# Sparse attention's entry in a new order: query latent, index keys, index queries, then the second key-value tile

## The reference

```
c_q, c_kv, k_idx, w_idx = split(h @ w_in, [256, 512, 576])       # 256 + 256 + 64 + 8 columns
c_q  = rms_norm(c_q, q_norm_g);  c_kv = rms_norm(c_kv, kv_norm_g)
q     = (c_q @ w_uq)    -> 16 heads of 64
q_idx = (c_q @ w_qidx)  -> 8 index heads of 64
k_idx = layer_norm(k_idx, g, b)
for each block of 128 queries:
    score = sum over heads of w_idx * relu(q_idx . k_idx)         # keys up to the query
    idx   = the 128 keys with the largest score
    attention of the 16 heads over those keys, keys and values made from c_kv
```

## Time and profile before

| | |
|---|---|
| median of three runs | 1538.74 us |
| the profiled execution, in all | 1539.63 us |
| its span, first to last instruction | 1537.8 us |
| PE busy | 1391.5 us, 90% |
| DVE busy | 851.6 us, 55% |
| ACT busy | 533.9 us, 35% |
| mean granted clock of PE, full speed is 1 | 0.952 |
| attention's entry, first latent tile to the first masked score | 878.3 to 1004.8 us |

### The profile page before, as it was taken

How to read it: one execution, slowest core, us unless ns; L and a number is a source line. 1 busy time by engine, 2 the same in 40 slices (tenths; PEclk the granted TensorE clock), 3 DMA queues, 4 the chain that set the end, 5 groups by cost and what they waited for, 6 DMA issues and landing times. The chain is left out here.

```text
span 1537.8 us, 17933 instructions
## 1 busy us (share of the span) xinstructions
PE 1391.5 (90%) x6983; PEld 1121.7 (73%) x6983; DVE 851.6 (55%) x1384; ACT 533.9 (35%) x956; POOL 171.3 (11%) x171
## 2 busy tenths in 40 slices
PE   5798889889879999999998696889989999999997
PEld 5676767779768878887886474646767888888885
DVE  4679899647454654555545538966453323332335
ACT  2353522445342222221223434557343222221321
POOL 0013230004310000000001101220010000000002
PEclk9899999899989999999999798889999999999999
DMA  9443412110404545554532120010102223322321
GB/s 330 142 164 111 162 56 83 56 55 1 164 28 155 201 139 189 185 196 166 167 121 69 33 71 28 28 56 2 55 28 82 82 82 110 110 82 82 110 73 65
DMA packets 102854, 158.36 MB, mean 103 GB/s; under 512 B 9326, under 2 KB 74107, under 8 KB 102779
## 3 DMA queue, kind: packets, MB, share of 16 engines
q1 hardware_dynamic: 91898, 115.40, 22.6%
q0 software_dynamic: 10880, 41.95, 7.8%
HBM read 155.24 MB, written 2.10 MB: 102 GB/s over the span
## 5 line engine op out<-in xcount | busy, mean ns | idle before, releaser
L396 PE MATMUL ps<-h_hi,w_hi 128*128 128x512 f32 x960 | 389.6, 406 | 6.4 <-DVE h_lo L824 6.4
L397 PE MATMUL ps<-h_lo,w_hi 128*128 128x512 f32 x960 | 382.7, 399 | 0.0
L398 PE MATMUL ps<-h_hi,w_lo 128*128 128x512 f32 x960 | 382.2, 398 | 0.0
L380 DVE TENSOR_TENSOR w_lo<-raw,w_hi 128x1024 fp32r<-128x1024 f32 x172 | 210.7, 1231 | 265.9 <-ACT w_hi L374 265.6
L374 ACT ACTIVATE w_hi<-raw 128x1024 fp32r<-128x1024 f32 x180 | 187.9, 1049 | 150.4 <-PE ps L1935 142.9
L396 PEld LDWEIGHTS ps<-h_hi,w_hi 128*128 128x128 f32 x960 | 183.9, 192 | 50.5 <-issue 9.0
L397 PEld LDWEIGHTS ps<-h_lo,w_hi 128*128 128x128 f32 x960 | 184.0, 192 | 43.2 <-issue 1.7
L398 PEld LDWEIGHTS ps<-h_hi,w_lo 128*128 128x128 f32 x960 | 183.2, 191 | 43.6
L448 DVE SCALAR_TENSOR_TENSOR ada_acc<-ada_in,c_act,ada_acc 128x512 f32<-128x512 f32 x147 | 112.8, 768 | 3.9
L1933 PE MATMUL ps<-w_hi,g_hi 128*128 128x512 f32 x256 | 101.6, 397 | 2.6 <-DVE w_lo L380 2.6
L1800 ACT ACTIVATE g_hi<-tmp 128x512 fp32r<-128x512 f32 x44 | 27.8, 632 | 211.9 <-DVE tmp L1835 211.9
(11 more groups left out here) (369 smaller groups left out, 2059.9 us busy)
## 6 DMA issues: line engine op xcount, KB each, us to landing
raw<-in_ffn_w_in_dram SPq DMA_DIRECT2D x44, 1024.0 KB, 5.1
ada_in<-in_ada_w_dram POOLq DMA_DIRECT2D x40, 1024.0 KB, 5.6
raw<-in_ffn_w_out_dram SPq DMA_DIRECT2D x20, 1024.0 KB, 5.0
raw<-in_gdn_w_in_dram SPq DMA_DIRECT2D x16, 1024.0 KB, 5.7
ada_in<-in_ada_w_dram SPq DMA_DIRECT2D x4, 1024.0 KB, 7.3
x_t<-in_x_dram SPq DMA_DIRECT2D x2, 2048.0 KB, 9.8
early_slab<-in_ada_w_dram SPq DMA_DIRECT2D x4, 1024.0 KB, 12.4
raw<-in_gdn_w_out_dram SPq DMA_DIRECT2D x4, 1024.0 KB, 5.0
```

Of the source, the lines that this page charges most:

```text
L380: ops.tensor_tensor(lo, raw_tile(s, kc) if src is None else src, f32(hi), ALU.subtract).then_inc(lo_done, 1)
L396: nc.tensor.matmul(out_, hi[:, k, :], r_hi[:, k, :], start=k == 0, stop=False)
L397: nc.tensor.matmul(out_, hi[:, k, :], r_lo[:, k, :], start=False, stop=False)
L398: last = nc.tensor.matmul(out_, lo[:, k, :], r_hi[:, k, :], start=False, stop=k == kc - 1)
```

## The change

PE makes tiles 0 and 1 only, then the small product with the query latent's statistics after its fourth chunk, the first broadcast, tile 2 with the small transposes in its middle, the index queries (now in banks 0, 1, 3 and 6), the key transposes, and tile 3 (into bank 2) with the first six logits of block 1 between its products and two behind it. The statistics of the key-value latent (into bank 0 instead of 4) follow; its broadcast (bank 1 instead of 5) moves into `dsa_q_pe`, behind the first query tile. That tile now waits for the variance (`row_made`) and for the last split of quad `Q_DSA + 1`. The logits of block 2 move behind the fourth query tile, those of block 3 behind the fourth key tile. ACT and DVE take the same order: block 1's relus and scores stand before the key-value latent's statistics and before its last weight split. POOL waits for that split before its own four. The buffer of the index queries moves to the second half of the key buffer, and block 0's mask is copied last. The diff, cut to its core (the moved calls at the end of the programs are as told here):

```diff
-        qi_t = fixed("qi_t", [P, 4, S], at=h_base)
+        qi_t = fixed("qi_t", [P, 4, S], at=k_at + 8192)
...
+        STAT_BANK, ROOT_BANK = [4, 0], [5, 1]
...
-        LAST = {3: 4 * Q_DSA + 6, 11: 4 * Q_DSA + 8, 18: 4 * Q_DSA + 9, 19: 4 * Q_DSA + 10, 35: 4 * Q_DSA + 12}
+        LAST = {3: 4 * Q_DSA + 5, 11: 4 * Q_DSA + 8, 18: 4 * Q_DSA + 9, 19: 4 * Q_DSA + 10, 35: 4 * Q_DSA + 12}
         def proj_ready(act, t):
...
+        QI_BANK = [0, 1, 3, 6]
+
         def dsa_in_pe(pe, m):
-            for s in range(4):
+            for s in range(2):
                 pe_tile(pe, Q_DSA, s, h_hi, h_lo, ready=(lambda k: h_block_here(pe, m, k)) if s == 0 else None)
-                if s == 2:
-                    pe_stats(pe, 0, sq_lat[:, 0, :, :], LC)
             pe.wait_ge(lo_done, 4 * Q_DSA + 5)
             w = [t[:, 0, 0:DC * SMALL].rearrange("p (k n) -> p k n", n=SMALL) for t in (w_hi, w_lo)]
             for k in range(DC):
                 last = mm3(ps[0:SMALL, 6, :], w[0][:, k, :], w[1][:, k, :], h_hi[:, k, :], h_lo[:, k, :],
                            k == 0, k == DC - 1)
+                if k == 3:
+                    pe_stats(pe, 0, sq_lat[:, 0, :, :], LC)
             last.then_inc(tile_done, 1)
             pe_bcast(pe, 0)
-            pe.wait_ge(sem("small_out"), 2)
-            for b in range(NB):
-                last = nc.tensor.transpose(ps[:, 7, b * SMALL:(b + 1) * SMALL], kx_t[0:SMALL, b * P:(b + 1) * P],
-                                           ident[0:SMALL, 0:SMALL])
-            last.then_inc(sem("small_turned"), 1)
+
+            def small_turn(k):
+                if k != DC // 2:
+                    return
+                pe.wait_ge(sem("small_out"), 2)
+                for b in range(NB):
+                    last = nc.tensor.transpose(ps[:, 7, b * SMALL:(b + 1) * SMALL], kx_t[0:SMALL, b * P:(b + 1) * P],
+                                               ident[0:SMALL, 0:SMALL])
+                last.then_inc(sem("small_turned"), 1)
+
+            pe_tile(pe, Q_DSA, 2, h_hi, h_lo, ready=small_turn)
             pe.wait_ge(sem("lat_made"), LC)
             pe.wait_ge(lo_done, 4 * Q_DSA + 6)
             wq = [t[:, 1, :].rearrange("p (k n) -> p k n", k=LC) for t in (w_hi, w_lo)]
             for j in range(4):
-                pe.wait_ge(sem("sq_made"), SQ_BASE[0] + j + 1)
                 for k in range(LC):
-                    last = mm3(ps[:, j, :], wq[0][:, k, j * P:(j + 1) * P], wq[1][:, k, j * P:(j + 1) * P],
+                    last = mm3(ps[:, QI_BANK[j], :], wq[0][:, k, j * P:(j + 1) * P], wq[1][:, k, j * P:(j + 1) * P],
                                cq_hi[:, k, :], cq_lo[:, k, :], k == 0, k == LC - 1)
                 last.then_inc(tile_done if j == 3 else sem("proj_mm"), 1)
-            pe_stats(pe, 1, sq_lat[:, 1, :, :], LC)
             pe.wait_ge(sem("small_made"), 2)
             for b in range(NB):
                 last = nc.tensor.transpose(ps[:, 7, b * P:(b + 1) * P], kn[:, b, :], ident[:, :])
             last.then_inc(sem("small_mm"), 1)
-            pe_bcast(pe, 1)
-
-        def indexer_pe(pe, b):
+
+            def first_logits(k):
+                if k >= 2:
+                    indexer_logit(pe, 1, k - 2)
+
+            pe_tile(pe, Q_DSA, 3, h_hi, h_lo, before=lambda: pe.wait_ge(sem("sq_made"), SQ_BASE[1] + 1),
+                    ready=first_logits, to=2)
+            for j in (6, 7):
+                indexer_logit(pe, 1, j)
+            pe.wait_ge(sem("proj_out"), AT_QI + 1)
+            pe_stats(pe, 1, sq_lat[:, 1, :, :], LC)
+            pe.wait_ge(sem("proj_out"), AT_QI + 2)
+
+        def indexer_logit(pe, b, j):
             n = (b + 1) * P
-            if b == 1:
-                pe.wait_ge(sem("lat_made"), 2 * LC)
+            t = (b - 1) * IH + j
+            if t == 0:
                 pe.wait_ge(sem("small_out"), 3)
                 pe.wait_ge(sem("proj_out"), AT_QI + 4)
+            if t >= 4:
+                pe.wait_ge(sem("relu_made"), t - 3)
+            lanes = slice(64 * (j % 2), 64 * (j % 2) + 64)
+            nc.tensor.matmul(ps[:, 4 + t % 4, 0:n], qi_t[lanes, j // 2, b * P:(b + 1) * P],
+                             kn_t[lanes, 0:n], start=True, stop=True).then_inc(sem("logit_mm"), 1)
+
+        def indexer_pe(pe, b):
             for j in range(IH):
-                t = (b - 1) * IH + j
-                if t >= 4:
-                    pe.wait_ge(sem("relu_made"), t - 3)
-                lanes = slice(64 * (j % 2), 64 * (j % 2) + 64)
-                nc.tensor.matmul(ps[:, 4 + t % 4, 0:n], qi_t[lanes, j // 2, b * P:(b + 1) * P],
-                                 kn_t[lanes, 0:n], start=True, stop=True).then_inc(sem("logit_mm"), 1)
+                indexer_logit(pe, b, j)
         def dsa_q_pe(pe):
             for j in range(8):
-                if j < 4:
-                    pe.wait_ge(sem("proj_out"), AT_QI + j + 1)
+                if j == 4:
+                    indexer_pe(pe, 2)
                 if j >= 4:
                     pe.wait_ge(sem("proj_out"), AT_Q + j - 3)
-                if j == 0:
+                elif j == 0:
+                    pe.wait_ge(sem("row_made"), 19)
                     pe.wait_ge(lo_done, 4 * Q_DSA + 8)
+                elif j == 1:
+                    pe_bcast(pe, 1)
+                    pe.wait_ge(sem("lat_scaled"), 2 * LC)
...
+                elif j == 2:
+                    pe.wait_ge(sem("sq_made"), SQ_BASE[1] + 2)
+                else:
+                    pe.wait_ge(sem("proj_out"), AT_QI + 3)
...
         def dsa_keys_pe(pe):
...
+                if j == 4:
+                    indexer_pe(pe, 3)
...
+                if j == 0:
+                    pe.wait_ge(sem("lat_made"), 2 * LC)
...
+        def latent_out(act, s, done, bank):
+            act.wait_ge(tile_done, 4 * Q_DSA + done)
+            nc.scalar.activation(latent[:, s // 2, s % 2, :], ps[:, bank, :], ACT.Copy).then_inc(sem("lat_here"), 1)
+            nc.scalar.activation(sq_lat[:, s // 2, s % 2, :], ps[:, bank, :], ACT.Square).then_inc(sem("sq_made"), 1)
         def dsa_in_act(act):
-            for s in range(4):
-                act.wait_ge(tile_done, 4 * Q_DSA + s + 1)
-                nc.scalar.activation(latent[:, s // 2, s % 2, :], ps[:, s, :], ACT.Copy).then_inc(sem("lat_here"), 1)
-                nc.scalar.activation(sq_lat[:, s // 2, s % 2, :], ps[:, s, :], ACT.Square).then_inc(sem("sq_made"), 1)
+            for s in range(2):
+                latent_out(act, s, s + 1, s)
...
-            act.wait_ge(tile_done, 4 * Q_DSA + 5)
+            act.wait_ge(tile_done, 4 * Q_DSA + 3)
...
+            latent_out(act, 2, 4, 2)
+            dsa_split_act(act, 1, 2, (tile_done, 4 * Q_DSA + 4))
...
-                nc.scalar.activation(qi_t[:, j, :], ps[:, j, :], ACT.Copy).then_inc(sem("proj_out"), 1)
+                nc.scalar.activation(qi_t[:, j, :], ps[:, QI_BANK[j], :], ACT.Copy).then_inc(sem("proj_out"), 1)
...
-            latent_hi_act(act, 1)
+            relu_act(act, 1)
+            latent_out(act, 3, 6, 2)
+            dsa_split_act(act, 1, 3, (tile_done, 4 * Q_DSA + 6))
+            for s in (0, 1):
+                dsa_split_act(act, 2, s)
         def latent_hi_act(act, half_):
...
         def dsa_qkv_act(act, nxt):
-            relu_act(act, 1)
-            for s in (0, 1):
-                dsa_split_act(act, 2, s)
-            relu_act(act, 2)
...
+                if j == 1:
+                    latent_hi_act(act, 1)
+                if j == 4:
+                    relu_act(act, 2)
...
-            relu_act(act, 3)
...
+                if j == 4:
+                    relu_act(act, 3)
...
-                nc.vector.scalar_tensor_tensor(tmp[:, k, :], ps[:, 5, :], qn_g[:, half_, k:k + 1],
+                nc.vector.scalar_tensor_tensor(tmp[:, k, :], ps[:, ROOT_BANK[half_], :], qn_g[:, half_, k:k + 1],
...
         def dsa_in_dve(dve, ch):
-            for s in range(4):
+            for s in range(2):
...
-                if s == 2:
-                    dve_var(dve, 0, LAT)
+            dve_var(dve, 0, LAT)
...
-                ch(nc.vector.tensor_tensor(kn[:, :, a * DH:(a + 1) * DH], k_x,
-                                           ln_gb[:, 1, :].unsqueeze(1).to_broadcast([P, NB, DH]), ALU.add))
-            nc.vector.tensor_copy(mask[:, 0, 0:P], causal[:, :]).then_inc(sem("small_made"), 1)
+                ins = nc.vector.tensor_tensor(kn[:, :, a * DH:(a + 1) * DH], k_x,
+                                              ln_gb[:, 1, :].unsqueeze(1).to_broadcast([P, NB, DH]), ALU.add)
+                if a == 0:
+                    ch.inc(ins)
+                else:
+                    ins.then_inc(sem("small_made"), 1)
+            ch.wait()
+            dsa_split_dve(dve, 1, 2)
+            score_dve(dve, ch, 1)
...
+            dsa_split_dve(dve, 1, 3)
...
+            ch(nc.vector.tensor_copy(mask[:, 0, 0:P], causal[:, :]))
         def score_dve(dve, ch, b):
...
+            pool.wait_ge(lo_done, 4 * Q_DSA + 8)
...
```

(14 more changed lines are left out.)

## The result

The changed kernel takes 1545.33 us (median of 13 runs, 1541.0 to 1548.4) against 1538.7 (13 runs, 1534.84 to 1540.96) for the kernel before: ratio 1.0043, 95% interval 1.0031 to 1.0054. In a second comparison it came again: 1547.17 against 1539.38, 1.0056 (1.0044 to 1.0068). The changed kernel is slower by 6.6 to 7.8 us, where 1.5 us faster was forecast, and it lies outside the range of 1532.3 to 1541.8.

What follows compares the result with a forecast made beforehand. DVE's serial choice of keys was taken as the bound; score 3 at 960.4 plus 6.3 put the double round at 966.7, 1.5 us earlier than 968.14. From the 1538.74 median that gave 1537.2 us, range 1532.3 to 1541.8.

Steps and rivals of the forecast that it cites:

- 3.4 us stall before the first query tile: PE idle from 923.0 to 926.4, waiting for DVE's split of the last weight quarter, with half clock taken behind it.
- DVE's own wait before score 3: DVE, ready at 955.2, waits 5.2 us for PE and ACT until score 3 starts at 960.4.
- Fourth tile with the eight logits: PE's fourth tile, 24 products at 5.6 us, plus eight logits at 0.28 each, 2.2 in all (1.6 to 4), ending at 920.2.
- eight slow and ten fast: The 18 products from 932.0: eight at half clock, 3.4 us, and ten at full clock, 2.3, ending at 937.7.
- the late broadcast: Key-value latent's broadcast behind the first query tile: its readers done at 932.0 at half clock, 930.3 at full clock.
- rival B: Half clock through the 18 products, block 2's logits and next 24 products: 8.2 us, double round 6.8 later, 1545.5; chance 0.10.
- Later stages follow it one for one: Everything behind the double round's first MAX8 moves by as much as its start, forecast 1.5 us earlier.
- Rival C: POOL's splits hold DVE at the first round's end and score 2; costs up to 2 us, 1539.2; chance 0.10.
- Rival D: Second latent behind first scores costs what the scores gained; double round starts at 968, 1538.7; chance 0.05.
- Rival A: PE keeps its clock around the first query tile or regains it at once; gain 4.7 us, 1534.0; chance 0.20.

Runs made afterwards that it cites:

- e1: Changed kernel with block 1's eight logits in one piece behind the fourth tile instead of between its products: 1540.27 us, 1.0002 of the kernel before.
- b1: Kernel before the change, with only block 3's logits and relus moved among the key tiles, behind the fourth: 1542.78 us, 1.0018 of the kernel before.
- e9: Changed kernel plus twenty unread products in PE's waits, twelve behind the second statistics, eight behind the late broadcast: 1539.71 us, 0.9996 of the kernel before.
- e10: e7 plus nine unread products in PE's wait behind the second statistics: 1532.3 us, 0.9947 of the kernel before.
- e11: e10 plus 28 unread products in PE's wait for the double round, begun four rounds before its end: 1535.18 us, 0.9972 of the kernel before.
- changed again: The changed kernel, unaltered, measured a second time beside the kernel before on one chip: 1547.17 against 1539.38 us, 1.0056.
- e6: Changed kernel with the broadcast before the first query tile and ACT's value-weight splits behind the key copies: 1536.11 us, 0.9978 of the kernel before.
- e7: Changed kernel with broadcast before the first query tile, ACT's value-weight splits behind the key copies, logits in one piece: 1532.12 us, 0.9952 of the kernel before.

## Why the prediction was wrong

*Right:* what bounds the stretch and how to look at it. The end follows the double round's start; in front of it DVE waits for PE and ACT, as forecast, and the length of most later pieces was hit: 3.5 us for block 2's logits (3.5), 5.7 for the 24 products behind them (5.6), 5.9 for splits and UK copies (5.9), 6.0 and 0.3 for score 3. The new 3.4 us stall before the first query tile stands there with its length and the half clock behind it. DVE's own wait before score 3 was 2.6 us where some 5 were forecast, since the first round started 3.3 us late and POOL held the mask and score 2 for 2.2.

*The step that failed: "Fourth tile with the eight logits", 5.6 + 2.2 = 7.8.* It measured 11.0 (911.9 to 922.97). The tile was as forecast, the six logits between products cost 0.81 each instead of 0.28. The upper bound that I gave, 0.5, was the cost of a logit among logits; no row showed one among fast products, and the bound from the nearest row did not hold. PE came to this piece 0.5 earlier than forecast, so that what stands behind it comes 2.8 us late (second latent's variance 926.03, forecast 923.2; score 3 963.23, forecast 960.4), and -1.5 turns into +1.45. e1 undoes only this: its tile and logits take 8.1 (7.8 forecast), and 3.1 us come back.

*The clock piece, "eight slow and ten fast", 5.7 us, fits neither trace.* In the first all 18 products are fast, 4.4 us; in the second 14 are slow (933.65 to 939.8), 7.15 us, and that is nearly the whole of the 2.8 that it takes more to the double round (86.1 against 83.3). That the first trace's double round lies at 969.59, just where the forecast and the 2.9 of the logits put it (966.7 and 2.9), is therefore luck. Between the tile and score 3 three small misses cancel: the 18 products 1.3 shorter, the late broadcast with its readers 0.6 longer (932.0 forecast, 2.8 late makes 934.8, measured 935.39), and the first relu 0.5 later behind the key tiles (1.2 us behind PE's last product, forecast 0.7). Before the change such a slow stretch was mostly hidden, because DVE was the path; now PE's slow products reach the end. I put all of it into rival B with 0.10. B had the side right, and PE's line as the cause. Its mechanism, half clock through the logits of block 2 and the 24 products behind them too, is in neither trace (granted clock 1.00 in both from 940 on), and its price, 6.8, is near the measured 6.6 by accident: it left out the logits, and part of the loss lies elsewhere.

*Behind the double round* "Later stages follow it one for one" failed too. Both traces of the changed kernel, and those of e1 and b1, have 1.6 to 2.1 us more there; those of the other orders without added products have at most 0.4. In the first trace of the changed kernel, and in e1 and b1, some 1.5 of it comes in one place: behind a PE wait of 2.3 to 2.5 us near the end, in the last feed-forward part, the clock falls to 0.50. Before the change the same wait (2.41 us) is followed by full clock. The same window before, after, in e1 and in the second trace:

```profile
1505.00:1508.00 3.00, 3.00 (x15) 2.43 (x14) 1.48 (x4) 0.72 (x2) 0.54 (x1) 1.00 0.00 0
```

```profile
1505.00:1508.00 3.00, 3.00 (x9) 2.31 (x8) 0.69 (x1) 0.72 (x2) 0.00 (x0) 0.50 0.00 0
```

```profile
1505.00:1508.00 3.00, 3.00 (x11) 2.34 (x11) 0.69 (x1) 1.26 (x4) 0.00 (x0) 0.77 0.00 0
```

```profile
1505.00:1508.00 3.00, 1.12 (x5) 0.94 (x6) 1.35 (x3) 1.15 (x2) 0.00 (x0) 1.00 0.00 0
```

The second trace of the changed kernel has its wait there (2.31 us) at full clock, and its 1.9 us come elsewhere: some 1.6 of them between 1094 and 1101, where its granted clock is 0.50 to 1098 and 0.73 to 1102, against 0.83 and 1.00 before. So the equal 571.6 of the two traces is a coincidence of two different slow stretches. The code in both places is unaltered. That the edit makes such stretches more frequent is not shown; it does shift the time at which PE comes to these waits.

*The sum:* 1.8 to 4.6 in front, 1.9 behind, makes 3.7 to 6.5 for the two traces, with starts of the layer 0.4 and 2.1 earlier than before; the medians say 6.6 and 7.8. Both traces are of quick executions, 2.2 and 3.0 us below the medians of their runs (1543.14 and 1544.17). Those runs have no trace, but the mean granted clock goes with their time: in the first comparison it is 0.950 to 0.952 in the five quickest (1541.0 to 1543.1) and 0.947 to 0.950 in the eight others. Where in those runs the slow stretches lie stays open, and with it the rest of the sum.

*Rival C* was right that POOL's splits would fall on the first mask and score 2 (2.2 us in one trace, 4.1 in the other) and right that the wait for PE covers it. *Rival D* fell as the mechanism that it named: the first round does start earlier, by 0.8 us, and POOL's hold leaves score 3's add. *Rival A* did not happen by itself: behind the 3.4 us stall the clock is at half in both traces. Its two fall times, 2.4 and 1.5 us into the idle pieces, should read 2.6 and 1.3 by the earlier trace rows, which changes nothing in it. e9 makes A's clock by hand and comes to parity with the kernel before, not to A's 4.7 us gain, because the logits still cost their 3.2.

## What to carry to other kernels

When an edit moves the path from one engine to another, price the new path with that engine's worst rows, not its usual ones: PE's slow clock was nearly harmless while DVE was the path and cost up to 4.8 us (e9 against the second trace) when it wasn't. Keep single full-float32 products together and out of a run of fast-format products, as long as the form at hand behaves as this one (0.81 against 0.33 us). When a forecast lands on a measured time, check its pieces one by one, since here three misses cancelled. And when an order fills one engine's gap by making another's line longer, look at which wait is then last: here three small moves (broadcast first, splits off the line, logits in one piece) turned 0.4 to 0.6% slower into 0.5% faster with the same work.

## What the runs showed of the hardware

- A float32 product with 64 rows and 256 columns cost 0.81 us as two instructions between fast-format products and 0.33 in a row of its like (e1), at granted clock 1.00 in both.
- POOL's splits of 128x1024 held not only DVE's add (2.32 instead of 0.29 us) but a one-input operation (TENSOR_SCALAR, 2.33 instead of 0.42) and a series of SCALAR_TENSOR_TENSOR (8.68 instead of 4.54); MAX8 and MATCH_REPLACE8 ran beside it at their usual length. The Trainium skill's "SBUF — State Buffer", section "SBUF: two separate sides", says that operations with two SBUF inputs or in a two-port mode are held and others not. These traces agree for the add, the SCALAR_TENSOR_TENSOR and MAX8. For TENSOR_SCALAR no row names its mode; 128 columns more cost it 0.07 us (0.35, 0.42, 0.49 us for 256, 384, 512 columns) where they cost MAX8 0.13, so it goes through its columns faster, but that this is a two-port mode is not shown.
- Twenty products whose result nobody reads, placed in PE's waits (e9), brought the changed kernel from 1.0043 and 1.0056 of the kernel before to 0.9996. In the trace the work behind them ran at granted clock 1.00 (2.4 GHz) where it had been 0.50 (1.2 GHz) up to 934.5 or 940, which is worth 2.0 to 4.8 us of the 5.6 to 7.5. In e10 nine of them gave 1.9 us in the trace and nothing in the median. In e11 28 of them, which ran past the end of the wait, made e10 0.2% slower.
- Of one and the same PE wait near the end (2.2 to 2.5 us) three traces (changed, e1, b1) show granted clock 0.50 behind it, at a cost of some 1.5 us, and six (before, changed again, e6, e7, e9, e10) show 1.00. The length of the wait alone does not tell which it will be.
